# The first layer of a two-layer streaming encoder step, unrolled and laid out on a new slot plan

## The reference, cut to what matters

```python
for i in range(DEPTH):                         # DEPTH = 2, D_MODEL = 1024, D_FF = 2816
    hp = _rmsnorm(xp, norm_mix[i])
    qkv = h @ w_qkv                            # layer 0: q and k are rotated (rope)
    s = einsum('bqhd,bkhd->bhqk', q, k) * 64 ** -0.5
    p = softmax(where(allowed, s, -inf))       # chunk mask of 64
    a = p[:, :, 0] - lam * p[:, :, 1]          # two maps of one head
    o = rmsnorm(einsum('bhqk,bkhe->bqhe', a, v), subln_w) * (1 - lam_init)
    x = x + o.reshape(b, t, 1024) @ w_o
    x = x + swiglu(rmsnorm(x, norm_ffn[i]))
```

## Time and profile before

| | before |
|---|---|
| median of 3 runs | 1607.16 us (1603.75 to 1608.9) |
| profiled execution, own time | 1607.57 us |
| its span, first to last instruction | 1605.4 us |
| TensorE matmul busy | 1563.1 us (97%) |
| VectorE / ScalarE / GpSimd busy | 619.9 / 560.9 / 581.5 us |
| chain that ended last | TensorE 91%, VectorE 5%, ScalarE 1%, DMA 1% |

### The profile page before, as it was taken

One profiled execution on the slowest core, in us unless ns is written; L12 is line 12 of the kernel. 1 busy time (PEld: TensorE's weight loads), 2 busy tenths in 40 slices (PEclk: granted clock), 3 DMA queues, 4 the chain that ended last, 5 costly groups with the idle time before them and its releaser, 6 DMA issues.

```text
span 1605.4 us, 29879 instructions
## 1 busy us (share of the span) xinstructions
PE 1563.1 (97%) x11071; PEld 1476.8 (92%) x11071; DVE 619.9 (39%) x1091; ACT 560.9 (35%) x995; POOL 581.5 (36%) x276
## 2 busy tenths in 40 slices
PE   6999999999999999999999999999999999999996
PEld 5888888999999999999978888888999999999996
DVE  6667776451111111121366666665521111111212
ACT  4455545442222222222334444444332222232221
POOL 3333233334544444333322222221344455444331
PEclk9999999999999999999999999999999999999998
DMA  5322223122222222222211211111122222222222
GB/s 188 98 85 83 95 85 107 41 79 79 78 82 88 78 78 85 76 82 85 94 62 61 62 60 60 60 57 48 67 79 85 85 78 78 91 78 74 83 83 82
DMA packets 44628, 128.49 MB, mean 80 GB/s; under 512 B 5648, under 2 KB 10256, under 8 KB 44576
## 3 DMA queue, kind: packets, MB, share of 16 engines
q1 hardware_dynamic: 44576, 127.79, 23.6%
HBM read 111.21 MB, written 11.83 MB: 77 GB/s over the span
## 4 chain that ended last, share of the span: by engine, by line
PE 91%; DVE 5%; issue 2%; ACT 1%; DMA 1%; SPq 0%; DVEq 0%; ACTq 0%
PE ps L486 73%; PE sps L534 3%; PE ops L597 3%; PE tps L554 2%; PE sps L540 2%; PE sps L535 2%; PE sps L536 2%; PE sps L542 1%; PE ops L587 1%; DVE acc L1164 1%; DVE aug_l L1303 1%; DVE xT L1173 0%; PE tps L568 0%; DVE ptl L1269 0%; PE ops L604 0%
## 5 line engine op out<-in xcount | busy, mean ns | idle before, releaser
L1069 POOL TENSOR_TENSOR w_lo<-w_raw,w_hi 128x1024 fp32r<-128x1024 f32 (+1 forms) x199 | 469.4, 2359 | 922.2 <-ACT w_hi L787 922.2
L486 PE MATMUL ps<-xh,w_hi 128*128 128x288 f32 x2176 | 489.5, 307 | 18.5 <-DVE xl L1418 11.5
L486 PE MATMUL ps<-xl,w_hi 128*128 128x288 f32 x2176 | 468.7, 297 | 0.0
L486 PE MATMUL ps<-xh,w_lo 128*128 128x288 f32 x2176 | 468.3, 297 | 0.0
L486 PEld LDWEIGHTS ps<-xh,w_hi 128*128 128x128 f32 x2176 | 350.2, 191 | 20.4 <-issue 19.9
L787 ACT ACTIVATE w_hi<-w_raw 128x1024 fp32r<-128x1024 f32 (+1 forms) x200 | 208.3, 1042 | 451.7 <-PE ps L486 449.5
L486 PEld LDWEIGHTS ps<-xh,w_lo 128*128 128x128 f32 x2176 | 352.9, 190 | 0.0
L486 PEld LDWEIGHTS ps<-xl,w_hi 128*128 128x128 f32 x2176 | 352.8, 190 | 0.0
L866 ACT ACTIVATE pr<-sps,nmax 128x384 f32<-128x384 f32 (+3 forms) x160 | 85.9, 537 | 205.4 <-DVE nmax L1233 188.4
L486 PE MATMUL ps<-hh,w_hi 128*128 128x288 f32 x704 | 150.9, 295 | 0.0
L486 PE MATMUL ps<-hl,w_hi 128*128 128x288 f32 x704 | 150.8, 295 | 0.0
(11 more groups left out here) (154 smaller groups left out, 1768.6 us busy)
## 6 DMA issues: line engine op xcount, KB each, us to landing
w_raw<-w_units SPq DMA_DIRECT2D x184, 512.0 KB, 3.2
w_raw<-w_units SPq DMA_DIRECT2D x16, 384.0 KB, 2.8
qsw<-qsin SPq DMA_DIRECT2D x64, 72.0 KB, 2.0
xT<-x_in SPq DMA_DIRECT2D x8, 288.0 KB, 5.6
dk_out<-kf SPq DMA_DIRECT2D x8, 288.0 KB, 2.1
dv_out<-vf SPq DMA_DIRECT2D x8, 288.0 KB, 4.1
fk_out<-kf SPq DMA_DIRECT2D x8, 288.0 KB, 4.1
fv_out<-vf SPq DMA_DIRECT2D x8, 288.0 KB, 4.0
```

The source lines that it names most:

```text
L486: mm = nc.tensor.matmul(out[:, half, :], w[:, k, :], rhs[:, kt, half * HALF:(half + 1) * HALF], start=start and w is w_hi[slot] and rhs is ...
L1069: nc.gpsimd.tensor_tensor(w_lo[slot][:, 0:kts, :], w_raw[slot][:, 0:kts, :], w_hi[slot][:, 0:kts, :].bitcast(F32), ALU.subtract).then_inc( ...
```

## The change

- Layer 0 is written out (no loops) on all engines, over t = 0 to 24 * 8 + 63. Attention of a group starts 24 slots after the group and reaches over 39 slots: product with V for the prompt at 27, head norm sum at 34, `norm_o` at 36, `split_o` at 38 (before: 24, 28, 30, 32).
- Scores of the two maps are made together by `score_pair` at slots 2, 6, 10, 14, 18: six 64-row matmuls that alternate between the two halves of the partitions, then two mask multiplies. `weigh` becomes `weigh_first` and `weigh_second` (two reciprocals instead of one of two columns) three slots later.
- VectorE: rotation of K at slot 12 (before 13), `k_lo` at 14 (before 17, behind `take_q`), rotation of Q at 20, `q_lo` at 22. ScalarE: `split` in layer 0 at the first slot after a unit's start.
- WO in both layers: 14 runs instead of 12, three single-step runs instead of four. `prep` on VectorE at steps 52, 57, 59, 61, 63 and after the end; on ScalarE one step after each tile's last run.
- In the diff below, `diff_layer` and `wo_prep` are ScalarE's, the loop with `lead(u + q // KT)` is ScalarE's in layer 1, `wo_residuals` and `wo_finish` are VectorE's.
- `norm_sum` of the swiglu norm moves from the first unit (k = 6) into the second (k = 2). The one ahead of layer 1 moves from k = 6 of the first unit to its end.

```diff
-N_WO, N_IN, N_OUT, N_LAYER = 24, 36, 80, 88
+N_WO, N_IN, N_OUT, N_LAYER = 24, 38, 82, 90
+WO_STEPS = ([(j, 4 + j, k) for j in (0, 1, 2) for k in range(6)]
+            + [(j, j - 2, k) for j in (3, 4, 5) for k in range(7)]
+            + [(6, 0, k) for k in range(KT)]
+            + [(6 + t, t, 7) for t in (1, 2, 3)]
+            + [(6 + t, t, k) for t in (4, 5, 6) for k in (6, 7)]
+            + [(13, 7, k) for k in range(KT)])
...
+D_SCORE, D_WEIGH, D_TURN = (2, 6, 10, 14, 18), (5, 9, 13, 17, 21), (8, 12, 16, 20, 24)
+D_VT, D_PVS, D_PVP, D_HEAD_SUM, D_HEAD_NORM, D_SPLIT_O = 6, 13, 27, 34, 36, 38
+D_K, D_ROT_K, D_K_LO, D_Q, D_ROT_Q, D_Q_LO, D_V = 8, 12, 14, 16, 20, 22, 24
...
-                    if k == 6 and norm > 0:
-                        norm_sum(norm)
...
+            def score_pair(a, par, p):
...
+                if some(a * 10 + 2 * p):
+                    pe.wait_ge(exp_done, val(a * 10 + 2 * p))
...
+                for x, y, first in ((qh, kh, True), (qh, kl, False), (ql, kh, False)):
+                    for h in range(2):
+                        b = slice(64 * h, 64 * h + 64)
+                        nc.tensor.matmul(sps[:, h, 0:width(i)], x[par][b, q], y[par][b, k], start=first, stop=False)
+                d = 0 if i == 4 else i
+                for h in range(2):
+                    nc.tensor.matmul(sps[:, h, P * d:P * d + P], ident16, mask[DIFF], start=False, stop=True
+                                     ).then_inc(s_done, 1)
...
-                first_unit(u, n, prep_count(L, 0, 0), 2 * L).then_inc(w_used, 1)
+                first_unit(u, n, prep_count(L, 0, 0)).then_inc(w_used, 1)
                 if L == FOX:
-
+                    norm_sum(2)
                     pe.wait_ge(f_hi_done, 1)
                     pe.wait_ge(f_lo_done, 1)
                     pe.wait_ge(r_ready, 3)
...
                 for k in range(KT):
+                    if k == NORM_AT:
+                        norm_sum(2 * L + 1)
                     mm = slice_(u + 1, n + 1, k, xh, xl, k, k == 0, k == KT - 1)
...
+            def diff_layer():
+                scale_of_norm(0)
+                for t in range(SLOTS * G + len(WO_STEPS)):
+                    g, s = t // SLOTS, t % SLOTS
+                    if t % KT == 1 and t >= KT:
+                        lead(Num(t // KT))
+                    diff_attention(t)
...
+                    else:
+                        wo_prep(DIFF, t - SLOTS * G)
+
+            def wo_prep(L, q):
+
+                for k in range(KT):
+                    if WO_END[6 + k] + 1 == q or (k == KT - 1 and q == len(WO_STEPS) - 1):
+                        act.wait_ge(ps_read, N_LAYER * L + N_WO + 6 + k + 1)
+                        prep(2 * L + 1, Num(k))
...
+                    for q in range(SLOTS + 2 * KT, len(WO_STEPS)):
+                        if q % KT == 1 and q > 6 * KT:
+                            lead(u + q // KT)
+                        wo_prep(L, q)
                 lead(u + 8)
                 scale_of_norm(2 * L + 1)
...
+            def wo_residuals(L, q):
+
+                for j in range(WO_RUNS - 1):
+                    if WO_END[j] + 1 == q:
...
+                        residual(Num(N_LAYER * L + N_WO + j), Num(WO_STEPS[WO_END[j]][1]))
+                if q == WO_END[6]:
+                    clear_acc(2 * L + 1)
+                for k in range(5):
+                    if q == (52, 57, 59, 61, 63)[k]:
+                        prep(2 * L + 1, Num(k))
+
+            def wo_finish(L):
+                dve.wait_ge(w_used, U_LAYER * L + U_IN)
+                residual(Num(N_LAYER * L + N_WO + WO_RUNS - 1), Num(WO_STEPS[-1][1]))
+                for k in range(5, KT):
+                    prep(2 * L + 1, Num(k))
```

More of the change, by code:

```diff
@@ L445, in _ @@
             for L in (DIFF, FOX):
[L446 to L463, removed]
+                if L == DIFF:
+                    first_layer()
+                else:
+                    group(Num(0), first=True)
+                    group(Num(1), second=True)
+                    with sp.Fori(0, 3) as it:
+                        for par in range(2):
+                            group(Num(2 + par, 2, it))
+                    for n in range(KT):
+                        load_unit(Num(U_LAYER * L + U_WO + n))
+                        if n == 0:
+                            store_v(L, Num(6))
+                            load_vpast(L, Num(7))
+                        if n == 1:
+                            store_k(L, Num(7))
+                        if n == 2:
+                            store_v(L, Num(7))
                 with sp.Fori(0, FT) as it:
@@ L619, in attention @@
-                for tt in range(len(T_AT[L])):
-                    if T_AT[L][tt] == slot:
+                    if S_AT[FOX][jj] == slot:
+                        score(a, par, jj)
+                for tt in range(len(T_AT[FOX])):
+                    if T_AT[FOX][tt] == slot:
                         if tt == 0:
[L622 to L632, removed]
-                u, n = g * 3 + U_LAYER * L, g * 3 + N_LAYER * L
+                            pe.wait_ge(vr_done, val((a + (G + 1)) * 2))
+                        transpose_p(FOX, a, par, tt)
+                for h in range(2):
+                    if PVS_AT[FOX][h] == slot:
+                        pv_sample(FOX, a, h)
+                    if PVP_AT[FOX][h] == slot:
+                        pv_prompt(FOX, a, h)
@@ L691, in forget_cumsum, with wo @@
                 mm.then_inc(f_cum, 1)
-            def last_attention(L, par):
-                a = Num(7)
+            def wo(L, q):
                 u, n = U_LAYER * L + U_WO, N_LAYER * L + N_WO
[L698 to L726, removed]
@@ L728, in _ @@
+                mm = slice_(Num(u + q // KT), Num(n + j), q % KT, oh, ol, k, q == WO_OPEN[j], q == WO_END[j])
+                if q % KT == KT - 1:
+                    mm.then_inc(w_used, 1)
+                elif q == WO_END[j]:
+                    mm.then_inc(wo_done, 1)
             for L in (DIFF, FOX):
                 first_group(L)
[L730 to L733, removed]
@@ L1089, in group @@
                                             ).then_inc(f_lo_done, 1)
-                if not alone:
-                    v_lo(L, g - 1)
+                else:
+                    v_lo(FOX, g - 1)
                 lead(u + 1)
@@ L1327, in attention, with group @@
+                for t in range(len(T_AT[FOX])):
+                    if T_AT[FOX][t] == slot:
+                        p_lo(FOX, a, t)
+                for h in range(2):
+                    if PVS_AT[FOX][h] == slot:
+                        o_sum(FOX, a, h)
+                    if PVS_AT[FOX][h] + 2 == slot:
                         o_lo_sample(a, h)
-                    if PVP_AT[L][h] == slot:
+                    if PVP_AT[FOX][h] == slot:
                         o_lo(a, h)
-            def group(L, g, par, first=False, alone=False):
+            def group(g, par, first=False, alone=False):
@@ L1341, in group @@
-                    if slot == K_LO_AT[L]:
-                        k_lo(L, g, par)
-                    if slot == (2 * KT if alone else TAKE_Q_AT[L]):
-                        take_q(L, g)
-                    if slot == 17 and alone and L == FOX:
-                        forget_2()
-                    if slot == ROTATE_AT[1] and L == DIFF:
-                        rotate(g, 1)
-                    if slot == Q_AT[L]:
-                        q_lo(L, g, par)
-                        if L == FOX:
-                            aug_left(g)
@@ L1353, in group @@
-                take_v(L, g)
+                    if slot == K_LO_AT[FOX]:
+                        k_lo(FOX, g, par)
+                    if slot == (2 * KT if alone else TAKE_Q_AT[FOX]):
+                        take_q(FOX, g)
+                    if slot == 17 and alone:
+                        forget_2()
+                    if slot == Q_AT[FOX]:
+                        q_lo(FOX, g, par)
+                        aug_left(g)
+                take_v(FOX, g)
             def forget_1():
```

525 lines of the change are left out of this document (314 added, 211 removed).

## The result

| | before | after |
|---|---|---|
| median | 1608.03 us (1603.75 to 1609.97) | 1626.13 us (1623.93 to 1627.91) |
| profiled execution, own time (span) | 1607.57 (1605.4) | 1625.71 (1623.9) |

The account below looks back on a forecast made before the run. TensorE, with matmuls in flight for 97% of the span, was taken as the bound. 1607.6 - 13 (attention) + 18 (WO ends) + 0.6 (moved norm sum) + 2 + 1.5 (two starts) = 1616.7, 1617 us; range 1597 to 1632.

Parts of the forecast that it names:

- Part 3: End of WO, both layers: splits behind squares make TensorE wait 3.4 and 6.6 us; +18 us.
- Part 1: Layer 0's score pairs: six matmuls in one visit save 0.64 us per 384-column pair, 2.9 us a group.
- The middle: Score pair price with streams side by side but weight loads one after the other: 1.22 us, saving 0.64.
- the end with both halves side by side: Lower bound of the score pair's price: 1.01 us, saving 0.85, or 4.1 us a group.
- Part 2: Layer 0's groups: VectorE's held weighting delays slot 20's transposes 1.4 us, leaving 1.5 saved per group; attention -13 us.
- the forecast's bounds: Whole kernel: 1609 to 1630 us around the forecast, given a chance of 0.62.
- pairs with nothing side by side: Upper bound of the score pair's price: 1.55 us, saving 0.31, 1.6 us a group; whole kernel 1622.
- Part 4: Two starts: norm sum and forget matmuls ahead of layer 1, +2 us; layer 0's first score, +1.5 us.
- Pairs side by side and VectorE keeps up: Rival on layer 0's score pairs: savings of 23 to 33 us against +22, 1607 to 1597 us; chance 0.18.
- The splits come in time: Rival at the end of WO: +18 turns to about -7, whole kernel 1592 us; chance 0.12.
- Costly alternation: Rival on score pairs: alternating halves costs a full weight load each time, about 1638 us; chance 0.07.

Follow-up runs that it names:

- e1_tail: Kernel after, with ScalarE's weight splits of units 31, 32 and 33 moved ahead of squares at the end of WO, both layers: 1607.65 us.
- e4_starts: Kernel after, with group 0's `k_lo` behind the taking of q again and layer 1's norm sum back in the first unit (k = 6): 1622.16 us.
- e6_lock_rot: Kernel after, with GpSimd's subtraction waiting for the fourth weighting and the rotation of q two slots later, layer 0: 1605.6 us.
- e7_rot: Kernel after, with only the rotation of q two slots later in layer 0, without a wait on GpSimd: 1627.32 us in one execution.
- e2_lock: Kernel after, with only GpSimd's subtraction made to wait for VectorE's fourth weighting in each group of layer 0: 1611.06 us.

## Why the prediction was half right

- **Part 3, the end of WO: right, and undersized by 2.1 us a layer.** Waits of 3.4 and 6.6 were forecast, 3.54 and 6.67 came, both ended by `w_lo` at the slices named, and e1_tail takes them away by the order alone. The term that was mis-sized most is the clock: 1.7 was taken for each wait. Behind the first it is 0.34 x 5.0 = 1.7. Behind the longer one it is 0.32 x 9.01 = 2.9. That is 1.2 of the 2.1. The waits themselves are 0.2 longer, the wait of unit 34 is 0.54 instead of 0.3, and the 0.5 that fewer short waits were to save lay ahead of this stretch.
- **Part 1, the price of a pair: mis-sized, in the harmless direction.** The middle (1.22) was taken because the only row for short neighbours was of one half; 0.99 came, the end with both halves side by side (1.01). By the Trainium skill, TensorEngine Tiling (Array Packing), Key Properties, different tiles can run weight loads and matmuls in parallel; the trace agrees (173.99, x2 in both timelines). A pair of 384 saves 0.87 instead of 0.64. A group's work fell only by 3.2 instead of the 4.1 of that end. Groups take turns in what is lost between: in one the head norm sum inserts 1.35 us instead of 1.01 and the last score comes 0.5 late, in the next they are 1.7 and 0.15.
- **Part 2, the wait of slot 20: right in place and cause, wrong in size, and its consequence was left out. This is the step that failed.** 1.4 us were taken, by a sum that isn't laid out, with "2 if the halves run side by side" beside it; they did, and 2.05 came. What the subtraction held was the tiny multiplication ahead of the weighting, and not the weighting itself. The larger miss: Part 3 charged a low clock to a wait of about 2 us, and Part 2 didn't, for a wait of the same length in the same engine. In four of seven groups it came, 1.5 us each (33.8 against 32.35). Of the 7.4 us that the attention fell short, this is 6.0; the longer waits are some 4 more, the last group's wait (1.46, where 0.3 was charged) 1.2, and a wait of group 0's first transposes (1.06 idle at 58.95, also for a weighting) 1.2. Some 5 came back: 2.4 as TensorE's work, which fell by 3.2 a group instead of 2.9; the rest wasn't traced, but the first six WO units of layer 1, with the same shorter runs, took 1.5 less. That 1626 lies within the forecast's bounds (1609 to 1630) is luck: their upper part was meant for pairs with nothing side by side.
- **Part 4: right.** The first score's wait grew by 1.5 (2.80 against 1.31, rows 14); e4_starts shows 2.3 in the wait and the half clock behind it, 3.8 in all, more than the 1.5 charged, since it keeps the later slot of the first pair and so falls under the 1.31 of before. The score came at 44.34 and not near 42.8, since group 1 began 1.5 later. Ahead of layer 1 the forget matmuls start 2.77 us after the norm sum with 1.64 of it idle, as forecast, and the stretch is 1.1 us longer; no low clock followed:

```profile
785.62 1.13 PE L531 MATMUL sps<-acc,cstf 128*128 128x288 f32 x4
788.39 0.51 PE L725 MATMUL sps<-xh,f_hi 128*128 128x288 f32 x2 [1.64 <-ACT rs L883]
```

- **The rivals.** "Pairs side by side and VectorE keeps up" was given 1597 to 1607 with both WO ends still slow: e6_lock_rot is that case, 1605.6. Its condition was well named, that slot 20 doesn't wait, but VectorE's air (9.3 us a group) was no help as long as one held instruction stood in its order. "The splits come in time" was worth 25 us there; e1_tail, which brings them in time, gains 18.5. Costly alternation is out: a pair costs 0.99 in either order.

What stays open: why four of the six equal waits of 2.05 us in groups 2 to 7 were followed by half clock and two were not; in e7_rot it was five of six. No run varied the length of the wait alone.

## What to carry to other kernels

When a schedule gives up air on one engine, list every instruction of VectorE with two SBUF inputs, however small, that can start during a GpSimd subtraction (and, by the row at 185.78, wide ones with a single input), and ask which matmul hangs behind it. Here a wait on GpSimd's side, with the next held instruction moved away, took a group from 32.35 us to 30.61, or from 33.84 where half clock had followed. On an engine that works in order, don't queue work that has long been ready (a weight split) behind an instruction that waits for another engine. And once a stall of TensorE is charged with a low clock in one place, charge every stall of that length.

## What the runs showed of the hardware

- 64-row matmuls on different halves of the partitions pass one another in the queue: written as three and three, they start two by two (177.21, 177.50, 177.67), and a pair inserts 0.99 us where one map inserts 0.93.
- Stalls of 1.9 us (idle, as the rows give it) were followed by half clock in four of six groups of after and five of six of e7_rot. Those of 1.65 (group 0's attention, after and e7_rot), 0.73 to 1.11 (e2_lock, seven groups) and 0.51 (e4_starts) were followed by it in none, those of 3.4 and 6.5 us each time in after. Two shorter stalls close together, 1.26 and 1.31 us, ending 2.3 us apart, were followed by it in before (0.72 between 42 and 48 us).
- VectorE instructions behind a GpSimd subtraction of 2.4 us: a 128x1 multiplication of two SBUF inputs took 2.15 instead of 0.16 us, a 128x512 scaling of one SBUF input 2.06 instead of 0.49, a 128x1 reciprocal 0.16 as elsewhere.
